# First tile's product in halves, first expert's rows selected by TensorE, last mixer tiles and last experts reordered

## What is computed

```
hn = RMSNorm(h);  [u | q | k | v | g_pool | g_sb] = hn @ w_in            1024 x 4096
P  = multi-scale trailing means of u, mixed by 128 x 128 maps
S  = stick-breaking attention of normed q, k and v (8 heads of 64)
h  = h + (sigmoid(g_pool) * (P @ w_pool_out) + sigmoid(g_sb) * (S @ w_sb_out)) @ w_o
h  = h + sum over the top 2 experts of the top group: weight * (silu(x @ w_gate) * (x @ w_up)) @ w_down
     x = RMSNorm(h); router: 4 groups of 8 experts; expert: 1024 -> 512 -> 1024
```

## Time and profile before

| | us |
|---|---|
| median of 3 runs (lowest, highest) | 943.34 (941.81, 944.59) |
| the profiled execution | 944.84 |
| its span, first to last instruction | 942.6 |
| TensorE busy, share of the span | 828.6, 88% |
| VectorE busy | 269.3, 29% |
| ScalarE busy | 196.9, 21% |
| GpSimd busy | 133.6, 14% |
| bytes moved | 251.41 MB, mean 267 GB/s |

### The profile page before, as it was taken

The page is one execution under the profiler, slowest core; times in us unless marked ns, Lnnn a source line. Parts: engine busy times, 40 slices in busy tenths (PEclk is TensorE's granted clock), DMA queues, the critical chain, the costliest instruction groups (busy, mean ns, idle before and its releaser), DMA issues. The chain is left out here.

```text
span 942.6 us, 10773 instructions
## 1 busy us (share of the span) xinstructions
PE 828.6 (88%) x4578; PEld 519.3 (55%) x4578; DVE 269.3 (29%) x497; ACT 196.9 (21%) x336; POOL 133.6 (14%) x154
## 2 busy tenths in 40 slices
PE   4999998999999999997899987787877888687976
PEld 3777895679999999785434432222222333222322
DVE  4555138854313434355111110101010411001010
ACT  4423237846121313111000000000000000000000
POOL 5010061000000001210222211211111111112101
PEclk9999999989999999998699998989889989989998
DMA  9142216000203043964999999999999999999993
GB/s 321 28 141 90 90 58 226 2 2 1 105 31 134 1 179 139 404 251 154 368 413 410 410 410 410 415 406 415 413 411 410 417 415 413 409 411 416 407 416 119
DMA packets 51616, 251.41 MB, mean 267 GB/s; under 512 B 7433, under 2 KB 7481, under 8 KB 26992
## 3 DMA queue, kind: packets, MB, share of 16 engines
q1 hardware_dynamic: 39344, 228.92, 59.8%
q0 software_dynamic: 11184, 21.79, 7.9%
q10 hardware_dynamic: 1040, 0.00, 0.1%
HBM read 242.30 MB, written 15.59 MB: 274 GB/s over the span
## 5 line engine op out<-in xcount | busy, mean ns | idle before, releaser
L1377 PE MATMUL ps<-ring,xT 128*64 128x512 f32 x768 | 188.9, 648 | 50.7 <-DMA ring<-in_w_up_dram 49.7
L1377 PEld LDWEIGHTS ps<-ring,xT 128*64 128x64 f32 x768 | 60.4, 149 | 176.0 <-issue 112.0
L1767 DVE COPY hidT<-ps 128x256 f32<-128x256 f32 x32 | 13.6, 425 | 401.8 <-PE ps L1386 401.8
L1395 PE MATMUL ps<-high_ring,hidT 128*64 128x512 f32 x512 | 118.6, 604 | 7.2 <-DMA high_ring<-in_w_down_dram 2.4
L1070 PE MATMUL ps<-hnT_hi,ring_r 128*128 128x288 f32 x512 | 91.6, 296 | 0.1
L1377 PE MATMUL ps<-high_ring,xT 128*64 128x512 f32 x256 | 65.0, 667 | 18.8 <-DMA high_ring<-in_w_up_dram 18.8
L1070 PEld LDWEIGHTS ps<-hnT_hi,ring_r 128*128 128x128 f32 x512 | 75.9, 188 | 0.5 <-issue 0.5
L987 ACT ACTIVATE silu<-ps,rstd 128x256 f32<-128x256 f32 x32 | 15.2, 474 | 292.1 <-PE ps L1377 292.1
L1395 PEld LDWEIGHTS ps<-high_ring,hidT 128*64 128x64 f32 x512 | 40.6, 138 | 63.2 <-issue 60.7
L717 POOL DMA_INDIRECT out_y_dram<-yb,idx x32 | 50.3, 1572 | 147.0 <-ACT yb L991 143.2
L711 POOL DMA_INDIRECT xg<-hn_dram,idx x32 | 33.5, 1048 | 259.7 <-PE ps L1367 238.1
(11 more groups left out here) (281 smaller groups left out, 1032.3 us busy)
## 6 DMA issues: line engine op xcount, KB each, us to landing
high_ring<-in_w_down_dram SPq DMA_DIRECT2D x32, 2048.0 KB, 35.0
ring<-in_w_gate_dram SPq DMA_DIRECT2D x24, 2048.0 KB, 34.2
ring<-in_w_up_dram SPq DMA_DIRECT2D x24, 2048.0 KB, 35.2
high_ring<-in_w_gate_dram SPq DMA_DIRECT2D x8, 2048.0 KB
high_ring<-in_w_up_dram SPq DMA_DIRECT2D x8, 2048.0 KB
ring<-in_w_in_dram SPq DMA_DIRECT2D x7, 2048.0 KB, 8.7
ring<-in_w_o_dram SPq DMA_DIRECT2D x2, 2048.0 KB, 10.5
ring<-in_w_in_dram SPq DMA_DIRECT2D x2, 1024.0 KB, 8.1
```

What stands on the lines that cost most here:

```text
L1377: last = pe.matmul(out, xT[:, odd, k % (KD // 2), k // (KD // 2), :], w[:, k, :, s * F // 2:(s + 1) * F // 2], start=(k == 0), stop=(k == ...
L1395: last = pe.matmul(banks(6 + odd, 0, BANK, SLOTS, s * SLOTS), hidT[:, k % (KF // 2), k // (KF // 2), :], w[:, k, s * HALF_D:(s + 1) * HALF ...
```

## The change

- **First tile's product in halves.** The product with the gain, the high part and the low part of tile 0 are made for chunks 0 to 3 and 4 to 7 apart, and TensorE may start with the first half. VectorE normalises tile 2 before it takes tile 1, and the transposes of tile t + 1 are put inside tile t (before chunk 4 for tile 0, chunk 2 for the others) instead of those of t + 2 behind it.
- **Last mixer tiles by halves.** Tiles 3 and 4 of half 1 run by turns: chunks 0 to 3 of both, then 4 to 7 of both. Behind the first the upper rows of W_o are free (`half_used`), and SP loads down 0 and half of pair 3 there. To make the place for it the low and merged parts (`merged_lo`, `mergedT`) are two arrays each.
- **First expert's rows selected.** For each tile VectorE makes a 0/1 matrix of the rows that are in the first expert's slots (`slots_first`), TensorE multiplies h by it (`select_tile`), ScalarE copies the 64 rows out, TensorE transposes them, VectorE applies the gain, and the first wide product follows at once, before the tables of row numbers and weights are used. Gather 0 is gone; gather 3 waits for the transposes of expert 1.
- **Order of loads.** Pair 4 is issued ahead of down 2. Near the end pair 31 is issued ahead of down 29.
- **Last pair ahead of the last downs.** TensorE makes the last wide product before down product 30; the hidden rows of expert 30 get a place of their own (`hidT_last`).
- **Routing.** The two comparisons of `route` are one; the product with the token numbers goes to GpSimd (`mark_tokens`); logits and ranks of the last tile have banks of their own; slots are made tile by tile in a written order.

```diff
@@ -514,6 +544,12 @@
                     sp.dma_start(pairs[pair][:, m, :].rearrange("p (s m) -> p s m", s=2),
                                  source[0, e].rearrange("(s p c) n -> p s (c n)", s=2, c=KD // 2)).then_inc(done, 16)
 
+            def wide_half(e, s, done):
+
+                for m, source in enumerate((w_gate, w_up)):
+                    sp.dma_start(pairs[e % PAIR_RING][:, m, :].rearrange("p (s m) -> p s m", s=2)[:, s, :],
+                                 source[0, e].rearrange("(s p c) n -> s p (c n)", s=2, c=KD // 2)[s]).then_inc(done, 16)
+
             def down_matrix(e, place_of, done):
 
 
...
@@ -531,23 +567,31 @@
...
+
+            sp.wait_ge(half_used, 1)
+            load_down(0)
+            wide_half(3, 0, first_half_loaded)
             sp.wait_ge(o_made, 2 * TILES)
-            load_down(0)
-            load_wide(3)
+            wide_half(3, 1, pair_loaded[3])
             load_down(1)
+
+            sp.wait_ge(wide_made, 1)
+            load_wide(PAIR_RING)
+
             sp.wait_ge(weights_made, 1)
             load_down(2)
-
-            sp.wait_ge(wide_made, 1)
-            load_wide(PAIR_RING)
             for e in range(1, EXPERTS):
-                if e + PAIR_RING < EXPERTS:
+                if e + PAIR_RING < EXPERTS - 1:
                     sp.wait_ge(wide_made, e + 1)
                     load_wide(e + PAIR_RING)
                 if e <= EARLY:
                     sp.wait_ge(down_made, e)
                     load_down(e - 1 + DOWN_RING)
                 if EARLY <= e < EXPERTS - DOWN_RING:
+                    if e == EXPERTS - 2 * DOWN_RING:
+
+                        sp.wait_ge(wide_made, EXPERTS - PAIR_RING)
+                        load_wide(EXPERTS - 1)
                     sp.wait_ge(down_made, e + 1)
                     load_down(e + DOWN_RING)
 
...
@@ -684,17 +728,38 @@
...
+
+            def mark_tokens(t):
+
+                n = TOK_ROWS[t]
+                pool.wait_ge(hot_ready, t + 1)
+                pool.tensor_scalar(hot_token[0:n, t, :, :], hot[0:n, t, :, :], token[0:n, t:t + 1], None,
+                                   ALU.mult).then_inc(token_ready, 1)
+
...
+                store_h(t, 0)
+            for t in range(3):
+                store_h(t, 1)
+                if t >= 1:
+                    mark_tokens(t - 1)
+            store_h(3, 1)
+            mark_tokens(2)
+            store_h(4, 1)
+            mark_tokens(3)
+            mark_tokens(4)
 
 
             pool.wait_ge(hn_stored, 16 * 2 * TILES)
             pool.wait_ge(y_stored, 16 * 2 * TILES)
+            pool.wait_ge(eT_made, 1)
             pool.memset(xg[:, :, :], 0.0).then_inc(xg_init, 1)
             pool.wait_ge(xg_init, 1)
             pool.wait_ge(table_out, 1)
...
@@ -728,11 +793,11 @@
...
 
-            gather(0)
+
             gather(1)
-            for e in range(2):
-                reached(eT_made, e + 1)
-                gather(e + 2)
+            gather(2)
+            reached(eT_made, 2)
+            gather(3)
             for e in range(EXPERTS):
                 if e + 4 < EXPERTS:
                     reached(eT_made, e + 3)
...
@@ -778,16 +843,23 @@
...
             act.wait_ge(stat_ready, 2)
             act.activation(stat[:, 2, 7:8], stat[:, 2, 6:7], ACT.Sqrt)
             square_x(0)
             split_high("k", (0,))
-            high_hn(0)
+            high_hn_first(0)
             split_high("k", (1,))
+            high_hn_first(1)
             square_x(1)
             split_high("k", (2, 3))
+            square_x(2)
             high_hn(1)
-            square_x(2)
             square_x(3)
             high_hn(2)
             square_x(4)
...
@@ -975,6 +1047,8 @@
                         act.wait_ge(hms, t + 1)
                         act.activation(stat[0:n, 2, t:t + 1], stat[0:n, 1, t:t + 1], ACT.Sqrt).then_inc(hroot, 1)
 
+            act.wait_ge(rows_selected, 1)
+            act.activation(xg_first[:, :], ps[:, SELECT_BANK, :], ACT.Copy).then_inc(first_out, 1)
             act.wait_ge(route_a, 1)
             act.activation(eg[:, :, :], eg[:, :, :], ACT.Exp)
             act.activation(small[:, 1, :], small[:, 0, :], ACT.Exp).then_inc(route_e, 1)
...
@@ -1051,8 +1127,10 @@
                 for k in range(KD):
                     if t == 0 and k % 2 == 0:
                         pe.wait_ge(low_made, PIECES_BEFORE[name] + k // 2 + 1)
-                    if name == "k" and t == 0 and k == 4:
-                        turn_x_tile(1)
+                    if name == "k" and k == (4 if t == 0 else 2) and t + 1 < TILES:
+                        turn_x_tile(t + 1)
+                    if name == "k" and t == 0 and k == KD // 2:
+                        pe.wait_ge(hn_low, 1)
                     last = rows_of(ps[0:n, bank, :], hn_hi[:, k, c:c + n], hn_lo[:, k, c:c + n], high, low, k, k == 0,
                                    k == KD - 1)
                 last.then_inc(rows_made, 1)
...
@@ -1073,12 +1151,10 @@
 
             turn_x_tile(0)
             for t in range(TILES):
-                pe.wait_ge(hn_low, t + 1)
+                pe.wait_ge(*((hn_low, t + 1) if t else (half_low, 1)))
                 if t == TILES - 1:
                     pe.wait_ge(rows_out, 1)
                 project_tile("k", t, bank_of[t])
-                if t + 2 < TILES:
-                    turn_x_tile(t + 2)
             turn_past()
             for t in range(TILES):
                 if t < 3:
...
@@ -1322,29 +1401,87 @@
...
-            for t in range(TILES):
+            for t in range(TILES - 2):
...
-                if t >= 2:
-                    rank_tile(t - 2)
-                if t >= 3:
-                    table_tile(t - 3)
...
+                if t == 2:
+                    rank_tile(0)
                 mixer_rows(t, 1, range(6, KD))
-            turn_h(TILES - 1, 1)
-            route_tile(TILES - 1, 1, 2 * TILES)
-            rank_tile(TILES - 2)
+
+
+            mixer_rows(3, 1, range(1))
+            turn_h(3, 0)
+            mixer_rows(3, 1, range(1, 2))
+            turn_h(2, 1)
+            mixer_rows(3, 1, range(2, 4))
+            route_tile(2, 1, 7)
+            mixer_rows(4, 1, range(0, 2))
+            route_tile(3, 0, 6)
+            rank_tile(1)
+            turn_h(4, 0)
+            mixer_rows(4, 1, range(2, 4)).then_inc(half_used, 1)
+            table_tile(0)
+            mixer_rows(3, 1, range(4, 6))
+            rank_tile(2)
+            mixer_rows(3, 1, range(6, KD))
+            route_tile(4, 0, 8)
+            mixer_rows(4, 1, range(4, 6))
+            turn_h(3, 1)
+            mixer_rows(4, 1, range(6, KD))
+            route_tile(3, 1, 9)
+
...
+            def select_tile(t):
+
...
+                n = TOK_ROWS[t]
+                pe.wait_ge(sel_ready, t + 1)
+                for s in range(2):
+                    last = pe.matmul(banks(SELECT_BANK, 0, BANK, SLOTS, s * SLOTS), sel[0:n, (t - 1) % TILES, :],
+                                     h[0:n, t, s * HALF_D:(s + 1) * HALF_D], start=(t == 0), stop=(t == TILES - 1),
+                                     skip_group_check=True)
+                if t == TILES - 1:
+                    last.then_inc(rows_selected, 1)
+
+            select_tile(0)
+            table_tile(1)
+            turn_h(4, 1)
+            select_tile(1)
+            route_tile(4, 1, 10)
+            select_tile(2)
             table_tile(2)
-            rank_tile(TILES - 1)
-            table_tile(TILES - 2)
-            table_tile(TILES - 1)
+            rank_tile(3)
+            select_tile(3)
+            rank_tile(4)
+            select_tile(4)
+            table_tile(3)
+            table_tile(4)
+            pe.wait_ge(first_out, 1)
+            for c in range(KD // 2):
+                last = pe.transpose(banks(3, c * P, (c + 1) * P), xg_first[:, c:HALF_D:KD // 2], ident[:, :])
+            last.then_inc(eT_made, 1)
+            pe.wait_ge(pair_loaded[0], 32)
+            wide(1, 0, 0, xT_first[:, :, :, :])
 
 
             pe.wait_ge(weights_in, 1)
...
@@ -1367,63 +1504,53 @@
...
             for e in range(EXPERTS):
                 odd = e % 2
-                if e + 1 < EXPERTS:
+                if e + 2 < EXPERTS:
                     pair_there(e + 1)
                     wide(e + 2, 1 - odd, (e + 1) % PAIR_RING)
                 if e == LATE + 2:
                     pe.wait_ge(late_out, 1)
-                turn_hidden(e + 1, odd)
+                if e != EXPERTS - 2:
+                    turn_hidden(e + 1, odd)
                 if e + 2 < EXPERTS:
-                    pe.wait_ge(gathered[odd], 16 * (e // 2 + 2))
+
+                    pe.wait_ge(gathered[odd], 16 * (e // 2 + 1 + odd))
                     turn_x(odd)
+                if e == EXPERTS - 3:
+
+                    turn_hidden(e + 2, 1 - odd)
+                    pair_there(e + 2)
+                    wide(e + 3, odd, (e + 2) % PAIR_RING)
                 pe.wait_ge(down_loaded[e % DOWN_RING], 16 * (e // DOWN_RING + 1))
                 if e >= 2:
```

(59 more changed lines are left out.)

145 lines of the change are left out of this document (94 added, 51 removed).

## The result

The changed kernel took 941.9 us in the median (940.54 to 946.09, 20 runs), the kernel before 944.15 beside it: ratio 0.9979, interval 0.9969 to 0.9989. That is 2.0 to 2.25 us where 4.3 had been forecast.

The account below looks back on a forecast made before the run. Expert-matrix DMA stream taken as full from 469.13 us, so only its start and what follows its last byte can move. Front -3.1, middle -0.4, end -0.8 sum to -4.3: 939.0 us from 943.34; 8-in-10 range 935.5 to 943.6.

Parts of the forecast that it names:

- the chain to the restart of the stream: From the mixer's end to pair 4's issue: first wide product ends at 463.0 instead of 469.13, 6.1 us earlier.
- the clock: TensorE at tile 1 of the first stage: stays high over a 2.5 us wait, -3.1 us; if it falls, -1.2.
- the front: First projection tiles: tile 1 starts at 24.05 instead of 26.38, stage ends at 48.75; -3.1 us, ends -1.2 and -3.4.
- the middle: Mixer's end and first expert: restart 6.1 us earlier, but 5.1 and 0.6 us of transfers behind it; net -0.4 us.
- the end: Last pair, downs and scatters: pair 31 ahead of down 29, three scatters in a chain; -0.8 us, ends -2.3 and 0.
- the shorter wait: Before tile 1, TensorE waits 2.5 us; clock held after 2.71 us and fell after 2.95 elsewhere, so taken as kept.
- Rival A: Clock falls in tile 1 of the first stage as in the kernel before; gain 2.4 us, 940.9 us, chance 0.25.
- The mechanism of the middle: Early half leaves about 9 us of DMA hole before the restart; down 2 behind it costs 5.1 us.
- The chain of VectorE: Behind the last mixer addition: two routings of 3.3 us each end at 447.9, first-expert slots follow until 450.0.
- The step that failed: From slots at 450.0, selecting products 0.9, drain 0.2, copy 0.7, transposes 1.1, gain product 0.7: first wide product starts 453.8.
- The scatters bind: Kernel's end: last three scatters each wait for the one before, 5.26 us apart, ending at 941.7 against 942.6.
- The Trainium skill's rule on VectorE and GpSimd: Routing chain: two-input VectorE and GpSimd SBUF instructions exclude one another; would add up to 0.5 us, sum -3.8.

Follow-up runs that it names:

- e1: Kernel before with only the front's edits (tile 0 in halves, norm of tile 2 and transposes one tile ahead); ratio 0.9973 to the kernel before.
- e3: Changed kernel with the last loads and products in the order of the kernel before; ratio 1.0003 to the kernel before.
- e8: Changed kernel with reordered chain to the first wide product, pair 4 loaded by halves and six idle TensorE products; 936.89 us, ratio 0.9912 to the kernel before.
- e9: Changed kernel again, unaltered, timed in a later series; ratio 0.9966 to the kernel before.
- e12: Repeat of the changed kernel with reordered chain, pair 4 by halves and six idle products; 937.76 us, ratio 0.9911 to the kernel before.
- e2: Kernel before with the edits of front and end, without selected rows, mixer halves and moved load of pair 4; ratio 0.9960 to the kernel before.
- e4: Changed kernel, but down 0 and both halves of pair 3 wait for the mixer's end; ratio 0.9990 to the kernel before.
- e5: Changed kernel with first-expert slots of tile 3 before the last routing and tile 4's table product behind the transposes; ratio 0.9957 to the kernel before.
- e6: Changed kernel with pair 4 loaded by halves, the first behind eight of the first wide product's sixteen products; ratio 0.9957 to the kernel before.
- e7: Changed kernel with seven idle TensorE products, six behind the ranks of tile 3 and one behind tile 4's; ratio 0.9945 to the kernel before.
- e10: Changed kernel with only the table product of tile 4 moved behind the transposes of the first expert's rows; ratio 0.9964 to the kernel before.
- e11: Changed kernel with reordered chain to the first wide product and pair 4 by halves, no idle products; ratio 0.9927 to the kernel before.
- the third series: Unaltered changed kernel beside three variants (table product moved; chain reordered with pair 4 halved; that plus idle products); ratios 0.9966, 0.9964, 0.9927, 0.9911 to the kernel before.

## Why the prediction came out too high

Two things were reckoned too well: the chain to the restart of the stream, which is the step that failed, and the clock, which the forecast took as kept at the front. The second doesn't show in the changed kernel's own profile.

The sum of the profiled run, term by term: -2.8 at the front (the first pair's issue), +1.3 in the middle, -1.7 at the end, together -3.2, against -3.1, -0.4 and -0.8. The last pair's landing gives the middle: 912.49 and the 5.1 us of the down that went behind it are 917.6, 1.5 below 919.04, of which the front has 2.8.

**The front: right, by its own steps.** First projection 12.23 (forecast 12.0), tile 1 at 24.08 (24.05), the clock kept, 2.9 us at the stage's end (3.1). That the clock was kept is luck of this execution, though. Thirteen profiles have this front. In six of them (the changed kernel, e1, e3, e8, e9, e12) the clock stays high in tile 1 and the stage ends 24.8 us behind tile 1's start; in seven (e2, e4, e5, e6, e7, e10, e11) it falls and the stage ends 26.4 behind it. The first pair is then issued at 366.1 to 366.7 in the six and at 367.3 to 368.4 in the seven (369.47 in before), so the front gives about 3 us in the one case and 1 to 2 in the other. The waits before tile 1 are 2.19 to 2.23 us in the six and 1.89 to 2.20 in the seven: the forecast's reason for a kept clock, the shorter wait, doesn't hold. Rival A had 0.25 and occurred in more than half of the profiles; e9, the changed kernel again, is among those that kept the clock.

**The mechanism of the middle: right.** The hole is there, every us of the restart counts, and the down behind it costs 4.9 (forecast 5.1). The chain of VectorE was right too: the last `hot_b` is made at 444.64, which is 447.4 in before's time (forecast 447.9).

**The step that failed: "the last two selecting products at the low clock 0.9 and their drain 0.2, ScalarE's copy 0.7, beside it ... table product (0.6) ... 453.8".** Here are its parts, in before's time (2.8 added):

| step | forecast | measured | why |
|---|---|---|---|
| last `hot_b` | 447.9 | 447.4 | |
| first-expert slots of tile 4 made | 450.0 | 450.6 | `select_tile(3)`, 1.97 us, stands ahead of `rank_tile(4)` |
| selected | 451.1 | 452.6 | four instructions, 1.97, not two |
| transposes start | 451.8 | 454.5 | eight table instructions, 2.05, not 0.6 |
| wide product starts | 453.8 | 456.5 | |
| it ends | 463.0 | 465.0 | 8.44 instead of 9.2 |

The start is 2.7 late and the end 2.0; with the 0.3 that the front gave less, pair 4 is 2.3 late, and the middle is +1.3 instead of -0.4. The root is a misreading of two prices. I priced `select_tile` by lines of code, two products a tile, though the rows of before show twice as many instructions for fp32 (x16 for a half of eight products), and I used that count elsewhere; `select_tile(3)`, ahead of `rank_tile(4)`, got no time of its own. For the table the sum has 0.6, which is what one tile takes at the full clock, where two tiles at the low clock stand on the path. Before's trace has both:

```profile
441.89 0.61 PE L1316 MATMUL ps<-hot_token,slot_hot 128*128 128x32 f32 x4
...
446.58 2.05 PE L1316 MATMUL ps<-hot_token,slot_hot 128*128 128x32 f32 x8 [1.43 <-DVE slot_hot L1703]
```

e5 and e10 show by trace that this is a matter of order: 2.6 and 1.1 us off the start. They also show what the forecast didn't have: an earlier start at the low clock can give part of itself back in the product (9.87 and 9.11 us), so that it ends 26.2 us behind the mixer's end in e5 and 27.3 in the changed kernel. e11, with e5's order, gave nothing back (8.50), so this differs from execution to execution. Order, clock (e7) and halves (e6) together gain clearly: 0.9911.

**The end: undervalued.** The scatters bind as forecast, but 4.9 apart where 5.26 was taken from one row; that gives 0.7 more. e1 and e2 say 1.2 us, e3 and the changed kernel 2.3, for a term of 0.8; the intervals of both pairs overlap, so the size isn't sharp. The Trainium skill's figure (DMA: Bandwidth & Descriptors, Anatomy of one DMA: 2.0 us and bytes by 436 GB/s, an estimate of 2.6 us for the scatter) stays far from the 4.9 of this trace, and by it the chain would not have bound. The Trainium skill's rule on VectorE and GpSimd (SBUF — State Buffer, Who interferes with whom) cost nothing here that the trace shows: GpSimd's mark of tile 3 ran from 441.62 to 442.06, beside a wait of VectorE and one instruction with a single input, which is no test. The mark of tile 4 started at 444.74 together with VectorE's `sel` of tile 3, which has both inputs in SBUF; they took 0.48 and 0.24 us, against 0.44 for the other mark and 0.23 for the `sel` at 435.62.

**From the profiled run to the medians.** The forecast was -4.3, the profiled runs differ by 3.2, the medians by 2.25 and in the third series by 3.1. The changed kernel's profile is a favourable execution twice over. At the front the clock fell in seven of thirteen profiles, for 1.6 us. At the end the last wide product is on the path: eleven profiles have the new end, and it took 8.7 to 8.8 us instead of 7.09 in four of them (e6 to e9). In the changed kernel and in e9, the same program, it waited 1.96 and 1.98 us for its weights and took 7.09 and 8.78 us, and the third last scatter left at 924.70 and 926.47. An estimate by these shares: 7/13 of 1.6 and 4/11 of 1.7, together 1.5 us, which would make 1.7 of the profiled 3.2.

**What remains open.** Before's own shares aren't known: its single profile, and e1's with the same end, had the last product at 7.09. So the estimate isn't a measurement, and how often each case occurs is known only by these few profiles. Nor is the middle's cost sharp: 1.3 by the changed kernel's trace, 1.4 by those of e1 and e3, 2.8 by their medians. Not tested is the order of pair 4 and down 2 by itself, which puts the 4.9 us behind the restart, nor the selected rows without the moved loads; that the mis-sized chain is what turned the middle from a small gain into a loss rests on the traces, and the time of each repair alone (e5, e6, e10) isn't clear of the noise.

## What to carry to other kernels

Where a stream is full from one issue to the end, price an edit first by two numbers: when that issue comes, and how many bytes now lie behind it; bytes moved ahead of a hole only move the hole. Count instructions, not calls: on the chain that releases the issue, find in the rows how many instructions one call makes and at which clock they run, and put nothing on the in-order engine between the last input and the product that waits for it which isn't needed by it. When such a chain is sparse, reordering alone can be given back in part by the low clock; look also for the next hole behind the one that closes. And before a single profile is compared with a median, see in several profiles whether the clock met each product on the path in the same way.

## What the runs showed of the hardware

- The first wide product, 32 instructions, took 8.44 us (the changed kernel), 8.63 (e9) and 8.99 (e3) in one and the same order, 9.87 (e5) and 8.50 (e11) in another, by when the granted clock rose from its lower level; behind fillers that kept TensorE busy it took 7.09 in e7, e8 and e12.
- After waits of 1.96 to 2.00 us ahead of the last wide product the full clock held in three profiles (the changed kernel, e4, e10) and not in four (e6 to e9); after waits of 0.28 to 0.31 us it held in all four (e2, e5, e11, e12). Ahead of tile 1, waits of 1.89 to 2.23 us were followed by a kept clock in six profiles and a fall in seven. A wait of about 2 us didn't tell the clock here, so a forecast that takes it from one row has a spread of 1.6 to 1.7 us for each such place on the path.
- A scatter of 0.26 MB released the next one 4.7 to 5.1 us after its own issue in the eleven profiles with three in a row, and 5.23 to 5.26 in the three with two (before, e1, e3), with the queues of the weights running down or empty.
